# Another order for the first group of seven products, with the activation sums on one engine

## The reference

```python
def sqrelu_mlp(u, w1, w2):
    return jnp.square(jax.nn.relu(u @ w1)) @ w2
...
h = h + sqrelu_mlp(rmsnorm(h, mlp_norm_g[i]), m_w1[i], m_w2[i])
gate = jax.nn.sigmoid(rmsnorm(h, ple_norm_g[i]) @ ple_w_gate[i])
h = h + gate * (p[i] @ ple_w_proj[i])
```

## Time and profile before

| | us |
|---|---|
| median of 3 runs | 1145.68 |
| lowest and highest run | 1145.5, 1148.5 |
| the profiled execution, its own time | 1147.5 |
| its span in the profile | 1145.7 |
| PE busy | 1113.8 |
| DVE busy | 781.1 |
| ACT busy | 453.0 |
| POOL busy | 252.0 |

### The profile page before, as it was taken

One profiled execution on the slowest core, in us unless ns is written; L12 is line 12 of the kernel. 1 busy time (PEld: TensorE's weight loads), 2 busy tenths in 40 slices (PEclk: granted clock), 3 DMA queues, 4 the chain that ended last, 5 costly groups with the idle time before them and its releaser, 6 DMA issues.

```text
span 1145.7 us, 15225 instructions
## 1 busy us (share of the span) xinstructions
PE 1113.8 (97%) x5482; PEld 937.7 (82%) x5482; DVE 781.1 (68%) x1129; ACT 453.0 (40%) x796; POOL 252.0 (22%) x230
## 2 busy tenths in 40 slices
PE   7999999998999996999999999999999999999998
PEld 6788888987788885888888888888888888888887
DVE  5888988888644488766766676768777774564321
ACT  5566656666532313323222323543333432243100
POOL 6431322314200095235523550000000000010000
PEclk9999999999999998999999999999999999999999
DMA  7000000004143304333433324899898892111211
GB/s 276 20 19 19 18 18 18 18 1 185 37 129 111 128 19 165 147 136 140 184 147 139 137 115 161 313 404 357 286 293 289 288 298 77 37 37 56 83 39 45
DMA packets 61801, 154.41 MB, mean 135 GB/s; under 512 B 5040, under 2 KB 6064, under 8 KB 61744
## 3 DMA queue, kind: packets, MB, share of 16 engines
q1 hardware_dynamic: 61600, 153.12, 37.6%
q10 hardware_dynamic: 144, 0.52, 0.1%
HBM read 119.55 MB, written 34.08 MB: 134 GB/s over the span
## 4 chain that ended last, share of the span: by engine, by line
PE 84%; DVE 9%; POOL 3%; issue 2%; ACT 1%; DMA 0%; DVEq 0%; POOLq 0%; ACTq 0%
PE pair L1999 23%; PE pair L1978 22%; PE pair L2042 8%; PE pair L1721 8%; PE pair L1860 6%; PE pair L2019 4%; PE pair L1796 3%; PE pair L2055 2%; PE pair L1779 2%; PE pair L1767 2%; PE pair L1938 1%; DVE probs L1288 1%; DVE pT L1313 1%; PE pair L1908 1%; DVE probs L1306 1%
## 5 line engine op out<-in xcount | busy, mean ns | idle before, releaser
L1999 PE MATMUL pair<-uT 128*128 128x512 f32 x1176 | 266.7, 389 | 0.0
L1999 PEld LDWEIGHTS pair<-uT 128*128 128x128 f32 x1176 | 220.7, 188 | 45.8
L1118 ACT ACTIVATE uT<-wo_raw 128x1024 fp32r<-128x1024 f32 x63 | 64.1, 1054 | 104.8 <-PE pair L1999 89.6
L1562 DVE TENSOR_TENSOR uT<-wo_raw,uT 128x1024 fp32r<-128x1024 f32 x63 | 74.9, 1221 | 39.0 <-ACT uT L1118 38.8
L631 POOL TENSOR_SCALAR row_var<-row_ssq 128x1 f32<-128x1 f32 x24 | 4.6, 191 | 437.2 <-ACT hn L1015 430.4
L1721 PE MATMUL pair<-WA,xT 128*128 128x512 f32 x384 | 96.7, 402 | 0.4 <-DVE WA L1213 0.2
L1860 PE MATMUL pair<-WA,oT 128*128 128x512 f32 x384 | 90.2, 392 | 1.7 <-DVE WA L1364 1.2
L1860 PEld LDWEIGHTS pair<-WA,oT 128*128 128x128 f32 x384 | 71.2, 188 | 16.7 <-issue 1.4
L1721 PEld LDWEIGHTS pair<-WA,xT 128*128 128x128 f32 x384 | 71.1, 191 | 14.9 <-DVE WA L1213 0.7
L1978 PE MATMUL pair<-WA,WB 128*128 128x512 f32 x312 | 74.4, 396 | 3.4 <-ACT xr L1093 3.4
L888 ACT ACTIVATE probs<-probs,nmax 128x257 f32<-128x257 f32 x128 | 63.5, 500 | 34.8 <-DVE nmax L1293 34.8
(11 more groups left out here) (182 smaller groups left out, 2101.5 us busy)
## 6 DMA issues: line engine op xcount, KB each, us to landing
wo_raw<-in_m_w SPq DMA_DIRECT2D x53, 512.0 KB, 6.4
wo_raw<-hid_kept SPq DMA_DIRECT2D x36, 512.0 KB, 4.7
hid_kept<-RES SPq DMA_DIRECT2D x28, 512.0 KB, 2.6
emb<-in_m_w SPq DMA_DIRECT2D x20, 512.0 KB, 6.2
RES<-in_m_w SPq DMA_DIRECT2D x8, 1024.0 KB, 6.6
RES<-in_a_wqkv SPq DMA_DIRECT2D x12, 512.0 KB, 8.4
uT_f<-in_m_w SPq DMA_DIRECT2D x6, 1024.0 KB, 7.1
act_buf<-hid_kept SPq DMA_DIRECT2D x11, 512.0 KB, 4.8
```

The source lines that it names most:

```text
L1118: nc.scalar.activation(operand(t, which, HI), unit(t, which), ACT.Copy).then_inc(op_hi, 1)
L1562: nc.vector.tensor_tensor(operand(t, which, LO), unit(t, which), operand(t, which, HI).bitcast(F32), ALU.subtract).then_inc(op_ready, 1)
L1999: mm = nc.tensor.matmul(ps[4 * (j % 2) + m][:], operand(t, 0, s)[:, k, m * P:(m + 1) * P], operand(t, 1, r)[:, k, :], start=(g == 0 and k ...
```

## The change

The products of group 1 are made in the order P0, P5, P3, P1, P2, P4, P6 (`FIRST_ORDER`); the other groups keep theirs. P3 of group 1 has a pair of its own (pair[3]), which DVE adds to z12 with one more instruction. The joins of group 1 come in the order z11, z12, z22, z21 (`joined_after`), and the waits of PE, DVE, POOL and SP on `z_added`, `z_copied` and `zq_ready` follow. The four weight sums of group 1 get four places in wo_raw; their first is made behind z_ready 8. POOL's four T instructions go; DVE makes T1 in three steps, T3 in two steps from T2. T3's high part comes behind the last relu on ACT, T4's behind the high part of the third product. The diff, with unchanged lines and some declarations left out:

```diff
@@ -44,7 +44,8 @@
...
 T1, T2, T3, T4 = range(4)
-T_ORDER = (T1, T2, T4, T3)
+FIRST_ORDER = (0, 5, 3, 1, 2, 4, 6)
@@ -194,9 +192,7 @@
...
                   WB[:, 2048:4096].rearrange("p (s k n) -> p s k n", s=2, k=4))
-        sum_a = wo_raw[:, 4, :].rearrange("p (k n) -> p k n", k=4)
-        sum_b = wo_raw[:, 5, :].rearrange("p (k n) -> p k n", k=4)
-        first_sum = slot_oT_f[:, LO]
+        sum_a, sum_b, sum_c, sum_d = (wo_raw[:, k, :].rearrange("p (k n) -> p k n", k=4) for k in (4, 5, 6, 7))
         tsum = [WA_f[:, j, LO] for j in range(4)]
@@ -225,12 +221,20 @@
         def a_source(g, i):
-            sums = (first_sum if g == 1 else sum_a, sum_b, sum_a, sum_b)
+            sums = (sum_a, sum_b, sum_c, sum_d) if g == 1 else (sum_a, sum_b, sum_a, sum_b)
             return {0: lambda: w1_quadrant(g, 0, 0), 1: lambda: sums[0], 2: lambda: sums[1], 3: lambda: sums[2],
...
         def group_of(q):
-            return q // N1 + 1, q % N1
+            return q // N1 + 1, FIRST_ORDER[q] if q < N1 else q % N1
+        def joined_after(q):
+            g, i = group_of(q)
+            if g == 1:
+                return {5: ("z11", 1), 2: ("z12", 2), 4: ("z22", 3), 6: ("z21", 4)}.get(i, (None, 0))
+            return {3: ("z12", 1), 4: ("z22", 2), 5: ("z11", 3), 6: ("z21", 4)}.get(i, (None, 0))
@@ -522,9 +525,7 @@
...
             sp.wait_ge(z_ready, 8)
-            sp.wait_ge(t_step, 1)
-            sp.wait_ge(t_low, 1)
-            sp.wait_ge(t3_step, 3)
+            sp.wait_ge(t_sum, 1)
             load_w1(2)
@@ -533,7 +534,7 @@
...
                     load_w1(g + 2)
-                sp.wait_ge(zq_ready, 4 * (g - 1) + 2)
+                sp.wait_ge(zq_ready, 4 * (g - 1) + (3 if g == 1 else 2))
                 spill("z22", g)
@@ -557,7 +558,7 @@
...
-                    s, v = ((z_ready, 8), (z_ready, 8), (a_ready, NP - 2), (a_ready, NP - 2), (prod_done, NP - 2),
+                    s, v = ((a_ready, N1), (a_ready, N1), (a_ready, NP - 2), (a_ready, NP - 2), (prod_done, NP - 2),
                             (prod_done, NP - 2), (prod_done, NP - 1), (prod_done, NP - 1), (hid_ready, 1),
@@ -746,18 +747,6 @@
...
-            def u(s, khalf, thalf):
-                return u_quadrant(s, khalf, thalf).bitcast(F32)
-            pool.wait_ge(wo_half, 2 * NB)
-            pool.wait_ge(uT_ready, 2 * NB)
-            pool.tensor_tensor(WA_f[:, T4, HI], u(LO, 0, 1), u(LO, 0, 0), ALU.subtract).then_inc(t_low, 1)
-            pool.tensor_tensor(tsum[T3], u(LO, 1, 1), u(LO, 0, 1), ALU.subtract).then_inc(t3_step, 1)
-            pool.wait_ge(t3_step, 1)
-            pool.tensor_tensor(tsum[T3], tsum[T3], u(HI, 1, 1), ALU.add).then_inc(t3_step, 1)
-            pool.wait_ge(t3_step, 2)
-            pool.tensor_tensor(tsum[T3], tsum[T3], u(HI, 0, 1), ALU.subtract).then_inc(t3_step, 1)
             def join(m, g):
@@ -779,7 +768,7 @@
...
                 done = 4 * (g - 1)
-                pool.wait_ge(zq_ready, done + 2)
+                pool.wait_ge(zq_ready, done + (3 if g == 1 else 2))
                 join("m2", g)
@@ -1054,11 +1043,7 @@
...
             def t_hi_part(j):
-                if j == T3:
-                    act.wait_ge(t3_step, 3)
-                else:
-                    act.wait_ge(t_sum, T_ORDER.index(j) + 1)
+                act.wait_ge(t_sum, j + 1)
                 nc.scalar.activation(t_s[:, j, HI], tsum[j], ACT.Copy).then_inc(t_hi, 1)
             def a_hi_part(q):
@@ -1134,15 +1119,15 @@
...
                     a_hi_part(1)
+                if i == 7:
+                    t_hi_part(T3)
             for q in range(NP):
...
                     take(q - 1)
+                if q + 2 < NP:
+                    a_hi_part(q + 2)
                 if q == 0:
                     t_hi_part(T4)
-                if q == 1:
-                    t_hi_part(T3)
-                if q + 2 < NP:
-                    a_hi_part(q + 2)
                 if q >= NP - 2:
@@ -1469,45 +1455,53 @@
             def t1_second():
                 dve.wait_ge(t_step, 1)
-                dve.wait_ge(t_low, 1)
-                nc.vector.tensor_tensor(tsum[T1], tsum[T1], WA_f[:, T4, HI], ALU.add).then_inc(t_sum, 1)
+                nc.vector.tensor_tensor(tsum[T1], tsum[T1], u(LO, 0, 1), ALU.add).then_inc(t_step, 1)
+            def t1_third():
+                dve.wait_ge(t_step, 2)
+                nc.vector.tensor_tensor(tsum[T1], tsum[T1], u(LO, 0, 0), ALU.subtract).then_inc(t_sum, 1)
             def t2_first():
...
             def t2_second():
-                dve.wait_ge(t_step, 2)
+                dve.wait_ge(t_step, 3)
                 nc.vector.tensor_tensor(tsum[T2], tsum[T2], u(LO, 1, 1), ALU.add).then_inc(t_sum, 1)
+            def t3_first():
+                dve.wait_ge(t_sum, 2)
+                nc.vector.tensor_tensor(tsum[T3], tsum[T2], u(HI, 0, 0), ALU.subtract).then_inc(t_step, 1)
+            def t3_second():
+                dve.wait_ge(t_step, 4)
+                nc.vector.tensor_tensor(tsum[T3], tsum[T3], u(LO, 0, 0), ALU.subtract).then_inc(t_sum, 1)
             def t4_first():
...
             def t4_second():
-                dve.wait_ge(t_step, 3)
+                dve.wait_ge(t_step, 5)
                 nc.vector.tensor_tensor(tsum[T4], tsum[T4], u(LO, 1, 0), ALU.add).then_inc(t_sum, 1)
             def t_lo_part(j):
-                dve.wait_ge(t_hi, T_ORDER.index(j) + 1)
+                dve.wait_ge(t_hi, j + 1)
                 nc.vector.tensor_tensor(t_s[:, j, LO], tsum[j], t_s[:, j, HI].bitcast(F32),
...
-            def a_sum_part(q):
-                g, i = group_of(q)
+            def a_sum_part(g, i):
...
                     if g == 1:
-                        dve.wait_ge(wo_half, 2 * NB)
+                        dve.wait_ge(z_ready, 8)
                     add = nc.vector.tensor_tensor(dst, w1_quadrant(g, 0, 1), w1_quadrant(g, 1, 1), ALU.add)
...
                     dve.wait_ge(a_sum, 4 * (g - 1) + 1)
-                    if g == 1:
-                        dve.wait_ge(z_ready, 8)
                     add = nc.vector.tensor_tensor(dst, a_source(g, 1), w1_quadrant(g, 0, 0), ALU.subtract)
@@ -1525,26 +1519,31 @@
             def join_chains(q):
                 g, i = group_of(q)
-                if i < 3:
+                name, place = joined_after(q)
+                if name is None:
                     return
...
                 y, z, x = pair[2 if g % 2 == 1 else 3], pair[0], pair[1]
-                if i == 6:
+                buf = halves(z_buf[name])
+                if name == "z21":
                     dve.wait_ge(z_clipped, g)
-                    z21 = halves(z_buf["z21"])
-                    nc.vector.tensor_tensor(z21, y[:], z21, ALU.mult).then_inc(zq_ready, 1)
-                else:
-                    dve.wait_ge(z_copied, 3 * g)
-                    chain, name = {3: (z, "z12"), 4: (y, "z22"), 5: (x, "z11")}[i]
-                    buf = halves(z_buf[name])
-                    nc.vector.tensor_tensor(buf, chain[:], buf, ALU.add).then_inc(z_added, 1)
+                    nc.vector.tensor_tensor(buf, y[:], buf, ALU.mult).then_inc(zq_ready, 1)
+                    return
+                dve.wait_ge(z_copied, 3 * (g - 1) + {"z11": 1, "z22": 2, "z12": 3}[name])
+                chain = {"z12": z, "z22": y, "z11": x}[name]
+                if g == 1 and name == "z12":
+                    nc.vector.tensor_tensor(buf, pair[3][:], buf, ALU.add).then_inc(z12_part, 1)
+                    dve.wait_ge(z12_part, 1)
+                nc.vector.tensor_tensor(buf, chain[:], buf, ALU.add).then_inc(z_added, 1)
             def square_joined(q):
                 g, i = group_of(q)
-                if i not in (3, 4, 5):
+                name, place = joined_after(q)
+                if name in (None, "z21"):
                     return
-                dve.wait_ge(z_added, 3 * (g - 1) + i - 2)
-                buf = z_buf[{3: "z12", 4: "z22", 5: "z11"}[i]]
+                dve.wait_ge(z_added, 3 * (g - 1) + place)
+                buf = z_buf[name]
                 nc.vector.scalar_tensor_tensor(out=buf, in0=buf, scalar=0.0, in1=buf, op0=ALU.max,
@@ -1571,21 +1570,24 @@
...
                     t1_first()
+                    t1_second()
                 if i == 3:
-                    t1_second()
+                    t1_third()
                     t2_first()
...
                 if i == 5:
-                    a_sum_part(1)
+                    t3_first()
                     t4_first()
...
                     t_lo_part(T2)
-            a_sum_part(2)
-            a_lo_part(1)
-            t4_second()
+                    a_lo_part(1)
+                if i == 7:
+                    t3_second()
+            for i in (1, 2, 3):
+                a_sum_part(1, i)
             for q in range(NP):
@@ -1594,14 +1596,15 @@
...
                 if q == 0:
-                    a_sum_part(3)
+                    a_sum_part(1, 4)
+                    t_lo_part(T3)
+                    t4_second()
```

(36 more changed lines are left out.)

## The result

The changed kernel takes 1151.49 us (median of 21 runs, 1149.8 to 1154.1), the kernel before 1147.13 (median of 21, 1145.1 to 1149.4). The ratio is 1.0038, 95% interval 1.003 to 1.0047: slower by 0.38%, 4.36 us. The forecast was slower by 3.15 us, at 1149.5.

The account below looks back on a forecast made before the run. PE, busy 97% of the span, was taken as the bound. Second group's start = P1's 461.55 + 7.45 + 5.44 + 1.36 + 5.44 + 1.48 + 5.44 = 488.15 against 485.0: 3.15 us later, 1149.5 us; range 1143.5 to 1154.5.

Parts of the forecast that it names:

- (a): T sums: POOL's four go, DVE gets three more; without meetings nine cost 19.8 us, in place of up to 6.4 each.
- (b): DVE's order in the hidden stage: P0's operand ready before 433.4; its 6.2 us idle and 2.0 us slow clock go.
- (c): P3 behind three weight sums on DVE, taken in turn with POOL's joins: starts near 448.75, 4.5 us late.
- (d): P1's high part on ACT stands behind T4's, which needs DVE's last T step: P1 starts near 461.55.
- (e): P1 on PE, after an idle over 5 us: 2.0 us of slow clock charged.
- (f): P4, directly behind P2 in the same accumulators, waits for ACT's copy to z12: 1.36 us.
- (g): P6, directly behind P4, waits for DVE to add z22: 1.48 us.
- (h): POOL's joins of group 1 and ACT's copy end before the second group's P2: no cost, 0.5 us of slack.
- the fourth rival: POOL's m5 held for three DVE operations, second group's P2 3.8 us late: 1153 to 1155, chance 0.10.
- DVE keeps POOL out: POOL's joins let in only after three DVE operations: P1 starts 3.65 us sooner, about 1146, no change, chance 0.14.
- The joins don't hold DVE: POOL's four joins cost DVE nothing: P1 at 453.95, 7.6 us saved, 1141.9 or 1139.9, chance 0.12.
- no clock loss: The idle before P1 costs no clock: 2.0 us less, 1147.5, no change, chance 0.12.

Follow-up runs that it names:

- run 3: Changed kernel, but POOL's m1 (and m2, m6, m7 behind it) also waits for the third weight sum of group 1: 1152.87 us, ratio 1.0039.
- run 1: Changed kernel, but on ACT T4's high part comes behind P1's high part, DVE's list unchanged: 1145.86 us, ratio 0.9982 to the kernel before.
- run 2: As run 1, and on DVE the fourth weight sum, T3's low part and T4's second step come behind P1's low part: 1145.7 us, ratio 0.9977.
- run 7: Changed kernel without POOL's joins m1, m2, m6, m7 of group 0, one-column memsets keeping the signals: 1144.05 us, ratio 0.9956 to the kernel before.
- run 5: Kernel before, in the old product order, with DVE making all T sums and POOL's four T instructions deleted: 1145.73 us, ratio 0.9982.
- run 4: Changed kernel with 20 matmuls, their results overwritten by P1, put in the idle ahead of P1: 1149.92 us, ratio 1.0012 to the kernel before.
- run 8: Run 5 with one more wait on DVE, for POOL's m1 behind P1's low part: 1146.46 us, ratio 0.9987 to the kernel before.
- Run 9: Run 5 with T1 one tile earlier, DVE pausing until m6, m7 behind P2's low part, fourth weight sum earlier, T4's second step and high part later: 1138.08 us, ratio 0.9912.

## Why the prediction was right

**The range, the sign and the chain held.** The measured +4.36 us lie at the slow side of the forecast's 3.15, and 1151.49 inside 1143.5 to 1154.5, 2.0 us over the 1149.5. By its own steps:

- (a), (b): P0 without an idle, T steps of 2.28 us, the last square done at 434.9 (435.4 forecast; this execution's hidden stage ended 0.5 us sooner). Right.
- (c): P3 15.4 us after P0, both forecast (448.75 - 433.4) and measured (448.28 - 432.87). It was hidden, as run 3 shows.
- (d): P1 28.15 us after P0 forecast, 28.17 measured. The three causes were tested by runs: the place of T4's high part on ACT (run 1: P1 3.9 us sooner), T4's step and what stands beside it on DVE (run 2: the last wait of 0.95), the joins (run 7: 7.3). They overlap and do not add up.
- (e): the slow clock of P1 was sized at 2.0 us and took 8.34 - 5.44 = 2.9. **This is the term that was mis-sized**: 0.9 of the 1.2 us by which the sum fell short. I took one row for a constant: both misses of size, this and the base below, went the same way. Over all profiles here the loss after an idle of 3 us or more lies between 1.7 and 3.0 us.
- (f): P4 6.80 us after P2 forecast, 6.81 measured. (g): P6 6.92 after P4 forecast, 7.13 measured. (h): the second group's P2 did not wait: ACT's copy ended at 498.1 and P2 started at 499.7, a slack of 1.6 us where 0.5 was counted, so the fourth rival did not occur.
- The second, smaller miss was the base: 1145.7 of three runs and 1147.5 of the profile were both within the scatter about 1147.1, and I put the sum between them, at 1146.35 as base: 0.8 us too low.

The working took the joins and DVE in turn. That came out right in this kernel, where sum 2 and sum 3 each wait for the sum before; it was no rule, and cost the expectation of run 5. So that part of the sum came out in part by luck. The rival *DVE keeps POOL out* did not occur here but is real: it is what happens in run 5. *The joins don't hold DVE* fell with run 7, *no clock loss* with P1's own 8.34 us and with run 4, where the same product at the same place takes 5.57.

## What to carry to other kernels

When an order of products changes, every engine's list has to change with it: the price of a step is read at what stands ahead of it in its queue, not at when its own inputs are ready. The same step, T4's high part on ACT, cost the changed kernel 6.7 us, of which 3.9 are P1's later start and 2.8 the clock behind it (run 1), and took back the gain of run 8. Removing an idle off the path brings nothing (run 3), and two parts of one change should be timed apart: here one part brought 3 to 4 us and the other, with its lists, took 7 to 8.

## What the runs showed of the hardware

Who gets the port that VectorE and GpSimd share was not what I expected. A POOL join was held through three DVE operations in the earlier trace rows, through six in run 5 (11.06 us instead of 2.4), through two in the changed kernel (m1, past the T step at 434.83 and sum 1). The later joins of the changed kernel, and those after the pause of run 8, were held by one each at most. These rows fit this: a DVE operation that is ready at once behind another keeps the port; POOL gets it when DVE pauses, be it for 0.04 us on a signal, and once DVE has itself waited, the two alternate. Run 9 does not fit: there m1 got in between two DVE operations without a pause between them. So the reading is not a rule, and what decides who is next stays open; it is drawn from the rows and the pause of run 8, not from a test of the port by itself. The Trainium skill (SBUF — State Buffer, "Who interferes with whom") states that whoever issues first gets the shared pair for the whole instruction and the other is fully blocked. That agrees with each single meeting, where the loser ends its own length after the other's end. Read as the order of asking it does not fit: run 5's m1 began at 437.86 and was held through five operations that began later. In the changed kernel, too, sum 1 (437.03) went ahead of m1 (434.99), and P3 was not the 2.1 us later that the strict reading in the prediction gave.

The loss by the lower clock shows no trend with how long PE had idled. After idles of 4.35 to 4.42 us alone it was 1.8 us (P1 of run 7), 2.5 (P3 of the changed kernel) and 3.0 (P3 of run 2); it was 1.7 after 3.3 and 2.7 after 3.6 (run 8), 2.9 after 4.7 (the changed kernel), 2.3 after 8.1 (run 5) and 2.5 after 11.4 (run 3). In the stretches no idle of 1.5 us or less was followed by a slow product; the product that follows only takes 0.1 to 0.2 us more (5.69 to 5.78 in place of 5.60).
